# The seam between two blocks of matmuls: a feed-forward's last down units and the next first unit, one token tile at a time

## The reference, cut to what matters

```
x = x + jnp.square(jax.nn.relu(h2 @ w_up[l])) @ w_down[l]                 # block one, width 4096
for l in range(2):                                                        # block two
    x = x + 0.5 * rms_norm(swiglu(rms_norm(x, ng[0]), w_gu, w_down), ng[1])   # width 2816
    h = rms_norm(x, ng[2])
    tok, qm = retention_mixer(h, ...) if l == 0 else mla_mixer(h, ...)
    x = x + rms_norm(concat(tok, memory_attention(qm, ...)) @ w_o[l], ng[3])
    x = x + 0.5 * rms_norm(swiglu(rms_norm(x, ng[4]), w_gu, w_down), ng[5])
```

## Time and profile before

| what | value |
|---|---|
| runs | 1471.94, 1473.89, 3533.91 us; median 1473.89 |
| profiled execution, span of the core | 1470.6 us (the page gives no other time of that execution) |
| PE busy | 1401.7 us (95%) |
| DVE, ACT, POOL busy | 922.4, 732.0, 192.7 us |
| mean granted TensorE clock | 0.982 |
| bytes read from HBM | 241.67 MB, 165 GB/s over the span |

### The profile page before, as it was taken

The page is one execution under the profiler, slowest core; times in us unless marked ns, Lnnn a source line. Parts: engine busy times, 40 slices in busy tenths (PEclk is TensorE's granted clock), DMA queues, the critical chain, the costliest instruction groups (busy, mean ns, idle before and its releaser), DMA issues.

```text
span 1470.6 us, 28247 instructions
## 1 busy us (share of the span) xinstructions
PE 1401.7 (95%) x11538; PEld 1358.3 (92%) x11538; DVE 922.4 (63%) x1368; ACT 732.0 (50%) x1205; POOL 192.7 (13%) x210
## 2 busy tenths in 40 slices
PE   5899899999999999999998999999999989899998
PEld 5878799999999999998898999999999987899998
DVE  7998786666535665556765665556564467565644
ACT  7712755544435454455446454455444364554443
POOL 0465000022000111013101111011110010111100
PEclk9899899999999999999999999999999989999999
DMA  9223324455554555544342555544555341345551
GB/s 372 105 103 116 127 86 174 159 204 185 194 185 160 177 195 191 195 173 155 135 144 99 190 197 189 198 172 172 188 198 199 146 170 58 109 178 195 192 200 58
DMA packets 36815, 244.33 MB, mean 166 GB/s; under 512 B 4208, under 2 KB 5360, under 8 KB 8816
## 3 DMA queue, kind: packets, MB, share of 16 engines
q1 hardware_dynamic: 34992, 238.17, 44.7%
q10 hardware_dynamic: 1728, 4.81, 0.9%
HBM read 241.67 MB, written 1.05 MB: 165 GB/s over the span
## 4 chain that ended last, share of the span: by engine, by line
PE 81%; DVE 9%; ACT 5%; issue 2%; POOL 2%; DMA 1%; SPq 0%; DVEq 0%; ACTq 0%; POOLq 0%
PE ps L1891 49%; PE ps L1931 26%; DVE wlo L1083 3%; PE ps L2114 1%; PE ps L2140 1%; ACT whi L592 1%; DVE alo L1478 1%; PE ps L2130 1%; DMA xtok<-in_xt 1%; POOL pr L1809 1%; POOL pr L1808 1%; PE ps L2019 1%; ACT junk L829 1%; DVE yr L1456 0%; ACT pP L782 0%
## 5 line engine op out<-in xcount | busy, mean ns | idle before, releaser
L1083 DVE TENSOR_TENSOR wlo<-raw,whi 128x1024 fp32r<-128x1024 f32 (+1 forms) x434 | 505.1, 1205 | 273.3 <-ACT whi L592 273.2
L1891 PE MATMUL ps<-ahi,whi 128*128 128x256 f32 x2112 | 599.5, 284 | 32.1 <-DVE wlo L1083 18.0
L592 ACT ACTIVATE whi<-raw 128x1024 fp32r<-128x1024 f32 (+1 forms) x434 | 427.2, 1032 | 368.8 <-PE ps L1931 188.1
L1891 PE MATMUL ps<-alo,whi 128*128 128x256 f32 x2112 | 595.4, 282 | 0.0
L1891 PE MATMUL ps<-ahi,wlo 128*128 128x256 f32 x2112 | 594.0, 281 | 0.0
L1891 PEld LDWEIGHTS ps<-ahi,whi 128*128 128x128 f32 x2112 | 403.1, 191 | 38.2 <-issue 23.5
L1891 PEld LDWEIGHTS ps<-alo,whi 128*128 128x128 f32 x2112 | 402.8, 191 | 0.7 <-issue 0.7
L1891 PEld LDWEIGHTS ps<-ahi,wlo 128*128 128x128 f32 x2112 | 401.9, 190 | 0.0
L1829 POOL TENSOR_TENSOR hlo<-fh,hhi 128x256 f32 (+3 forms) x104 | 86.1, 828 | 756.2 <-ACT hhi L899 545.5
L1538 DVE TENSOR_TENSOR fa<-ps,r 128x512 f32<-128x512 f32 x104 | 71.9, 692 | 171.1 <-PE ps L1891 170.9
L1931 PE MATMUL ps<-whi,hhi 128*128 128x256 f32 x960 | 149.1, 277 | 0.0
(11 more groups left out here) (350 smaller groups left out, 1362.9 us busy)
## 6 DMA issues: line engine op xcount, KB each, us to landing
raw<-in_w_gu SPq DMA_DIRECT2D x88, 1024.0 KB, 4.8
raw<-in_w_fd SPq DMA_DIRECT2D x44, 1024.0 KB, 4.8
raw<-in_w_up SPq DMA_DIRECT2D x16, 1024.0 KB, 4.8
raw<-in_w_dn SPq DMA_DIRECT2D x16, 1024.0 KB, 4.8
raw<-in_w_ret SPq DMA_DIRECT2D x13, 1024.0 KB, 4.8
raw<-in_w_mg SPq DMA_DIRECT2D x8, 1024.0 KB, 4.9
raw<-in_w_o SPq DMA_DIRECT2D x8, 1024.0 KB, 6.3
raw<-in_w_mem SPq DMA_DIRECT2D x4, 1024.0 KB, 4.7
```

The lines of the kernel that those rows point to most:

```text
L592: nc.scalar.activation(whi[:, m % SPL, c], raw[:, n % RAW, c], ACT.Copy).then_inc(S("w_hi"), 1)
L1083: ins = tt(wlo[:, m % SPL, c], raw[:, n % RAW, c], whi[:, m % SPL, c].bitcast(F32), ALU.subtract)
L1891: ins = mm(dst, lhsT, rhs, start=k == 0 and p == 0, stop=k == kt - 1 and p == len(pairs) - 1)
```

## The change

For q in `EARLY = (1, 2, 4, 5)` the last two down units (a, then b) and the first unit behind them are worked off by token tile. PE's order becomes: a tile 0, b tile 0 (`y_first`), a tile 1 (unit a is done), transposes of tile 0, b tile 1 in two halves of its output columns (`y_left` after the first), the old residual's transposes of tile 1, the first unit for the 128 tokens of tile 0, the rest of tile 1's transposes, the first unit for tile 1. The unit order of the last two down units is changed behind the last feed-forward too (q = 7). ACT and DVE get the order that belongs to it: the split of the first up unit moves behind the first tile's norm, the split of the unit behind it into the transition. `w_lo_left` tells PE that the left half of a unit's low part is there. Each SP load waits for the same `w_lo` as before, and each POOL instruction stands where it stood.

```diff
+EARLY = (1, 2, 4, 5)
+LATE_HALF = (1, 2, 4, 5, 7)
...
                 def squares_y(t):
-                    act.wait_ge(*y_ready(q, t))
+                    if t and q in LATE_HALF:
+                        act.wait_ge(S("y_left"), LATE_HALF.index(q) + 1)
+                    else:
+                        act.wait_ge(*y_ready(q, t))
                     for h in range(2):
+                        if t and h and q in LATE_HALF:
+                            act.wait_ge(*y_ready(q, t))
...
+                if q in EARLY:
+                    if post:
+                        squares_y(0)
+                        root_y(0)
+                    ahead(LAST_DOWN[q] - 1)
+                    high(0, 0)
+                    high(0, 1)
+                    if post:
+                        squares_y(1)
+                        root_y(1)
+                    ahead(LAST_DOWN[q])
+                    high(1, 0)
+                    high(1, 1)
...
                 def result(i, u):
-                    if u < ndn - 1:
+                    if u < ndn - 2:
                         weights(dn + u, i, UNIT)
...
+                    if q in EARLY:
+                        sum_y(0)
+                        scale_y(0)
+                        ahead(LAST_DOWN[q] - 1)
+                        low(0, 0)
+                        low(0, 1)
+                        sum_y(1)
+                        scale_y(1)
+                        low(1, 0)
+                        low(1, 1)
+                        ahead(LAST_DOWN[q])
...
+            def ffn_down(q, first, n_units, need, halfway):
...
+                a, b = n_units - 2, n_units - 1
+                pe.wait_ge(S("w_lo"), SPLIT_BEFORE[first + a] + 1)
+                need(a)
+                piece(a, 0, 0)
+                piece(a, 0, 1)
+                need(b)
+                pe.wait_ge(S("w_lo_left"), SPLIT_BEFORE[first + b] + 1)
+                piece(b, 0, 0)
+                pe.wait_ge(S("w_lo"), SPLIT_BEFORE[first + b] + 1)
+                piece(b, 0, 1).then_inc(S("y_first"), 1)
+                piece(a, 1, 0)
+                piece(a, 1, 1).then_inc(S("unit_split_done"), 1)
+                halfway()
+                piece(b, 1, 0, (0, 1))
+                piece(b, 1, 1, (0, 1)).then_inc(S("y_left"), 1)
+                piece(b, 1, 0, (2, 3))
+                piece(b, 1, 1, (2, 3)).then_inc(S("unit_split_done"), 1)
...
+            def first_unit(n, q, late):
...
+                for t, sem in enumerate(("t_lo_first", "t_lo")):
+                    xs = slice(t * P, t * P + P)
+                    if t:
+                        late()
+                    for c in range(2):
+                        for k in range(KT):
+                            if c == 0:
+                                pe.wait_ge(S(sem), 8 * q + k + 1)
+                            ws = slice(k * T + c * P, k * T + c * P + P)
+                            for p, (wgt, x) in enumerate([(whi, ahi), (whi, alo), (wlo, ahi)]):
+                                ins = mm(bank[:, c, xs], wgt[:, slot, ws], x[:, k, xs], start=k == 0 and p == 0,
+                                         stop=k == KT - 1 and p == 2)
...
+            def turn_early(q, t):
+                if q < FIRST_POST:
+                    new_residual(q, t, 0)
+                    new_residual(q, t, 1)
+                else:
+                    pe.wait_ge(S("x_new"), 4 * q)
+                    old_residual(t)
+                    new_term(q, t, 0)
+                    new_term(q, t, 1)
+
+            def turn_late(q):
+                if q < FIRST_POST:
+                    return lambda: (new_residual(q, 1, 0), new_residual(q, 1, 1))
+                old_residual(1)
+                return lambda: (new_term(q, 1, 0), new_term(q, 1, 1))
```

More of the change, by code:

```diff
@@ L1937, in down, with piece @@
                 assert n == LAST_DOWN[q]
-            def transposed(q):
[L1941 to L1953, removed]
+            def ffn_down(q, first, n_units, need, halfway):
+                def piece(u, t, kk, chunks=range(4)):
+                    n = first + u
+                    xs = slice(t * P, t * P + P)
+                    k = 2 * u + kk
+                    for p, (wgt, x) in enumerate([(whi, hhi), (whi, hlo), (wlo, hhi)]):
+                        for c in chunks:
+                            ws = slice(kk * D + T * c, kk * D + T * c + T)
+                            ins = mm(two(2 + 2 * t + c // 2)[:, c % 2], x[:, k, xs], wgt[:, n_slot(n), ws],
+                                     start=u + kk + p + c % 2 == 0, stop=u == n_units - 1 and kk == 1 and p == 2,
+                                     skip_group_check=True)
+                    return ins
+                for u in range(n_units - 2):
+                    pe.wait_ge(S("w_lo"), SPLIT_BEFORE[first + u] + 1)
+                    need(u)
+                    for t in range(TT):
+                        for kk in range(2):
+                            ins = piece(u, t, kk)
+                    ins.then_inc(S("unit_split_done"), 1)
+                a, b = n_units - 2, n_units - 1
[15 more added lines that the diff above has]
+                piece(b, 1, 1, (2, 3)).then_inc(S("unit_split_done"), 1)
+                assert first + b == LAST_DOWN[q]
@@ new lines, in old_residual, with new_term @@
+            def old_residual(t):
+                for k in range(KT):
+                    h, i = k // 4, k % 4
+                    mm(PS[turned(t, h)][:, i * P:i * P + P], xr[:, t, k * P:k * P + P], C["ident"], is_transpose=True,
+                       start=i == 0, stop=False, skip_group_check=True)
+            def new_term(q, t, h):
+                pe.wait_ge(S("y_new"), 4 * (q - FIRST_POST) + 2 * t + h + 1)
+                for i in range(4):
+                    k = 4 * h + i
+                    ins = mm(PS[turned(t, h)][:, i * P:i * P + P], yr[:, t, k * P:k * P + P], C["ident"],
+                             is_transpose=True, start=False, stop=i == 3, skip_group_check=True)
+                ins.then_inc(S("x_tr"), 1)
@@ L1957, in transposed @@
                         for h in range(2):
[L1958 to L1962, removed]
+                            new_residual(q, t, h)
                 else:
@@ L2189, in ffn @@
                 q = (0, 1, 3, 4, 6)[f]
-                need = transposed(q)
                 h0 = sum(x[3] for x in ffns[:f])
+                if q in EARLY:
+                    late = turn_late(q)
+                else:
+                    need = transposed(q)
                 def hidden(i, u):
-                    unit(up + u, ahi, alo, KT, i, need=need if i is None and u == 0 else None)
+                    if i is not None or u:
+                        unit(up + u, ahi, alo, KT, i)
+                    elif q in EARLY:
+                        first_unit(up, q, late)
+                    else:
+                        unit(up, ahi, alo, KT, need=need)
                     if i is None and u == 0:
@@ L2256, in turn_heads @@
                     ins.then_inc(S("ln_tr"), 1)
-                need = transposed(2)
-                unit(AT["w_ret", 12], ahi, alo, KT, need=need)
+                first_unit(AT["w_ret", 12], 2, turn_late(2))
                 token_roots(2)
@@ L2313, in job @@
                     ins.then_inc(S("lat_done"), 1)
-                need = transposed(5)
-                unit(u2, ahi, alo, KT, need=need)
+                first_unit(u2, 5, turn_late(5))
                 token_roots(5)
```

85 lines of the change are left out of this document (56 added, 29 removed).

## The result

The changed kernel takes **1495.7 us** (median of 4 runs, 1493.3 to 1497.6) beside 1476.1 of the kernel before (4 runs): ratio 1.014, 95% interval 1.0117 to 1.0164. One of the four runs of the kernel before took 3533.9 us; it is left out of the ratio, and the medians of 1473.9 to 1476.7 that the same kernel had beside the experiments bear out the 1476.1. The changed kernel is 19.6 us slower; 11.2 were forecast. The time lies inside the stated range, but 0.8% was forecast and 1.4% came. The profiled execution took 1497.6 us with a span of 1495.8.

A forecast was written before the change was run, and what follows sets the result against it. PE, busy 95% of the span, was taken as the bound. Terms +21.3 - 3.7 - 0.8 - 5.0 - 0.6 = +11.2 us on the profiled 1470.6 gave 1481.8, plus 3.3 to the runs' median: 1485 us, range 1475 to 1497.

The forecast's parts named there:

- No wait ahead of tile 0's half, the splits in time: Seams with a norm: PE never waits before tile 0's half, split slack 1 us; at q = 1, 0.5 us idle.
- The gap of 1.35 us in the middle: Between the first unit's halves PE idles 1.35 us, in place of 2.6: -3.7 us over three seams, -0.8 at q = 1.
- 0.113 us a pair: First unit's 128-column matmuls cost their weight load, as 24-column ones do: +5.3 us a seam, +21.3 for four.
- Rivals 1 and 3: Narrow pairs at the fp32 price, 1524 to 1528 us, chance 0.15; or priced by columns, 1466 us, chance 0.03.
- The 81 ns a pair: Skill's pace for 128-column load and matmul pairs: first unit 7.8 us, whole change about 1474, no change at all.
- The end, -0.6: At q = 7 tile 0's norm is done 2.7 us earlier against the last matmul: -0.6 us.
- The clock, -5.0: The 1.65 us lost to 1.2 GHz behind idle time at three of four seams is all won back: -5.0 us.
- the window at 142 us: Profile window of the 24-column matmuls, granted clock 1.00, cited as a sign that narrow pairs keep the clock up.
- Rival 2: Clock stays low in the narrow stretches, one stretch at each seam: +18 us, 1492 us; chance 0.14.

The follow-up runs named there:

- experiment 6: Kernel before, with PE's idle time at seams q = 1, 2, 4 and 5 filled with unread 256-column matmuls: 1472.6 us beside 1476.7.
- Experiment 7: Changed kernel with 12 unread 256-column matmuls in the 1.35 us gap between the first unit's halves, at four seams: 1489.2 us beside 1476.7.
- Experiment 3: Changed kernel, but in the first unit one tile's activations are stationary and 256 weight columns move (result layout not undone): 1476.4 us beside 1475.9 of before.

## Why the prediction was wrong

The steps in their order:

- **No wait ahead of tile 0's half, the splits in time**: right at q = 2, 4 and 5. At q = 1 the half starts 0.4 us after b tile 1, where 0.5 was said. That DVE's split would be longer beside POOL's sums was not seen; its slack of 1 us took it.
- **The gap of 1.35 us in the middle**: right, at all four seams.
- **0.113 us a pair**: right, 0.112. The row of the 24-column matmuls gave the price: with 128x128 blocks of 4-byte weights, 24 columns, 128 columns and (at 0.113 to 0.118) 256 columns cost about the same here. Rivals 1 and 3 are out. The 81 ns a pair that the prediction took from the Trainium skill (TensorE: Matmul & The Clock Gate, "Back-to-back issue gap") is not what these pairs take; the measurement decides. (The estimate after it sums to 1473, not 1474.)
- **The end, -0.6**: from the start of the last matmul to the end of the span it is 0.8 shorter (6.48 beside 7.26), but the last two down units took 0.4 longer. -0.4 in all.
- **The clock, -5.0: this step failed**, and by it the prediction. "I take all of it back" was half of the truth. The three stretches of 3.4 us behind the old idle time did go. But the text took the window at 142 us as evidence that narrow matmuls keep the clock up. It was weak evidence: one stretch of one profile, and in the profile of experiment 6 the clock fell among the same matmuls. Nor did it show what happens around a short gap. The gap of 1.35 us that the same text had found was the place. Where a stretch begins there, it lasts 10.2 us and not 3.4, since the pairs behind it don't end it: T is 2.65 and 2.86 us longer than in the filled kernel at q = 2 and 5, and the wide unit behind takes 1.7 and 1.5 us more. That is 8.8 us in this profile, where the sum had 0, so the term came to about +3.8 where -5.0 stood. Forecast 11.2 and 8.8 make 20.0, and 19.6 were measured. That it fits so closely is luck: 19.6 is a difference of medians, while the spans of the two profiled executions are 25.2 us apart. Of the rest, 2.6 us stand ahead of the first down product (375.2 beside 372.6) and 1.9 in the slower pace of the fourth feed-forward (last section). Rival 2 named the effect, and the idle 1.35 us in the middle of the narrow pairs with it, at 18 us in all, but by stretches of 3.4 us at every seam, and with a chance of 0.14.

Experiment 7 bears out that the failed term is the miss: with the gap filled the four seams have T of 17.2 and 18.4 us, and the kernel takes 1489.2 beside 1476.7, +12.5 (interval 7.5 to 15.8) where 11.2 were forecast.

Why was there nothing to win with this cut in the first place? A wide unit costs 5.5 us, each narrow half 5.3. What tile 0's half does in idle time is paid back in full, because tile 1's half then costs as much as the whole unit would have. The idle time of 2.6 us is no longer empty, and it is no shorter for the work that counts. Experiment 3 takes that price away and shows the second limit: the gap of 1.35 us in the middle stays, and `diag` comes late behind a split of 2.4 us on DVE. Whether that limit holds is open, since no run had `diag` ahead of the split.

What stays open: why the stretch began at two seams in one profile and at three in the other, and how the runs without a profile divide. The time of the changed kernel has ranged from 1493.3 to 1503.1, which is what one or two more of such stretches would make; no run here ties the two. And why the clock falls behind a gap among narrow pairs, behind none among wide ones, and near 144 us without any, no run here settles.

## What to carry to other kernels

Before a matmul is cut by its moving columns to start half of it sooner, ask what its weight load costs alone, from a row with the same weight block and few columns: if that is the pace of the wide one, the work done ahead is free but the rest costs as much as the whole, and only a cut that keeps the moving side wide can win (here it broke even). Then look for the short idle gap that is left, and at what stands behind it: in every long stretch here the narrow pairs ran on at half clock until wide matmuls came. Where a gap can't be removed, unread matmuls in it can pay (0.3 to 0.4% here). And before one window is taken as proof that the clock holds, look whether other profiles of the same place say so too.

## What the runs showed of the hardware

- With narrow fp32r pairs behind idle time the granted clock stayed at 1.2 GHz for 20.5 to 23.9 us, four times of four, and the same pairs behind filled idle time ran at 2.4 GHz, four times of four.
- The clock can fall with no idle time of PE above 0.1 us in the 12 us before: at 144.6 us in the profile of experiment 6 (before, filled), to 1.2 GHz for 13.7 us, among matmuls of 24 columns.
- DVE's difference of two SBUF tensors (128x1024, 1.18 us each) took 3.46 us for two beside POOL's sum of two SBUF tensors, which took 4.39 for two instead of 2.5; apart they took 2.36 and 2.51. The Trainium skill says so (GPSIMD Engine Reference, Specifications: the SBUF interfaces are shared with VectorE, with contention when a DVE instruction has two SBUF inputs), and the trace agrees. Beside `low`, of whose two tensor inputs one lies in PSUM, POOL's sums took 2.51 for two and `low` 2.15 for eight, where with POOL idle at q = 1 it had taken 4.23 for sixteen.
- The pace of the same down products is 0.113 us in most feed-forwards and 0.118 in some, with no half-clock stretch in them, and which ones it is differs between the two profiles of the changed kernel: the 432 matmuls ahead of unit a take 49.0 us in the second feed-forward and 50.9 in the fourth in the one, 50.9 and 49.0 in the other. It was not pursued; it moves the time by 2 to 3 us a feed-forward.
